# Two-block model on one core: squares of the norms added in pairs, one weighted moment for the final norm, and the first two units after a norm multiplied in parts

## The reference

```
y = x * rsqrt(mean(x*x) + EPS) * g            # EPS = 1e-6
h = y * (1 + scale) + shift                   # scale, shift from "ada" vectors
```

## Time and profile before

| quantity | value |
|---|---|
| median of 3 runs | 2177.64 us |
| the profiled execution, own time | 2177.91 us |
| its span (first to last instruction) | 2176.1 us |
| PE busy | 2119.0 us (97%) |
| DVE busy | 1749.7 us (80%) |
| ACT busy | 1334.7 us (61%) |
| mean granted TensorE clock | 0.988 |
| experts stage, from about | 1155 us |

### The profile page before, as it was taken

One profiled execution on the slowest core, in us unless ns is written; L12 is line 12 of the kernel. 1 busy time (PEld: TensorE's weight loads), 2 busy tenths in 40 slices (PEclk: granted clock), 3 DMA queues, 4 the chain that ended last, 5 costly groups with the idle time before them and its releaser, 6 DMA issues.

```text
span 2176.1 us, 33858 instructions
## 1 busy us (share of the span) xinstructions
PE 2119.0 (97%) x13613; PEld 1866.2 (86%) x13613; DVE 1749.7 (80%) x2143; ACT 1334.7 (61%) x1278; POOL 31.0 (1%) x60
## 2 busy tenths in 40 slices
PE   7999999999999999999999999999999999999998
PEld 5899999899999889999977888888888888888887
DVE  4978865877766878887878888888888888888887
ACT  3565554556645753434756776766777767776775
POOL 3000000000000000000000000000000000000000
PEclk8999999999999999999999999999999999999999
DMA  9777855566646548987456999999999999999995
GB/s 320 234 227 227 242 188 168 181 210 198 205 166 211 175 143 287 306 308 259 149 178 229 354 350 342 367 348 341 350 341 373 338 340 346 359 357 337 354 337 192
DMA packets 356160, 595.06 MB, mean 273 GB/s; under 512 B 10376, under 2 KB 201368, under 8 KB 356008
## 3 DMA queue, kind: packets, MB, share of 16 engines
q1 hardware_dynamic: 352864, 586.92, 78.7%
q0 software_dynamic: 2752, 5.86, 1.2%
q10 hardware_dynamic: 392, 0.13, 0.0%
HBM read 591.80 MB, written 4.22 MB: 274 GB/s over the span
## 4 chain that ended last, share of the span: by engine, by line
PE 83%; DVE 9%; ACT 3%; issue 3%; DMA 2%; SPq 0%; DVEq 0%; ACTq 0%
PE ps L1590 9%; PE ps L1592 9%; PE ps L1591 9%; PE ps L1119 6%; PE ps L1120 6%; PE ps L1121 6%; PE ps L1619 5%; PE ps L1620 5%; PE ps L1621 5%; PE ps L1144 2%; PE ps L1145 2%; PE ps L1146 2%; DVE wlo L1687 2%; DVE acc L1735 2%; ACT whi L701 1%
## 5 line engine op out<-in xcount | busy, mean ns | idle before, releaser
L1687 DVE TENSOR_TENSOR wlo<-raw,whi 128x2048 fp32r<-128x2048 f32 x485 | 1109.7, 2290 | 280.2 <-ACT whi L701 263.2
L701 ACT CAST whi<-raw 128x2048 fp32r<-128x2048 f32 x485 | 927.3, 1912 | 405.7 <-PE ps L1592 141.4
L1119 PE MATMUL ps<-hhi,whi 128*128 128x256 f32 x1424 | 411.3, 289 | 2.1 <-DVE wlo L1687 1.8
L1120 PE MATMUL ps<-hlo,whi 128*128 128x256 f32 x1424 | 403.4, 283 | 0.0
L1121 PE MATMUL ps<-hhi,wlo 128*128 128x256 f32 x1424 | 403.2, 283 | 0.0
L1590 PE MATMUL ps<-whi,xghi 128*128 128x512 f32 x896 | 364.1, 406 | 0.5 <-DVE wlo L1687 0.5
L1592 PE MATMUL ps<-wlo,xghi 128*128 128x512 f32 x896 | 353.9, 395 | 0.0
L1591 PE MATMUL ps<-whi,xglo 128*128 128x512 f32 x896 | 353.8, 395 | 0.0
L1119 PEld LDWEIGHTS ps<-hhi,whi 128*128 128x128 f32 x1424 | 273.5, 192 | 10.0 <-issue 7.0
L1120 PEld LDWEIGHTS ps<-hlo,whi 128*128 128x128 f32 x1424 | 273.6, 192 | 0.3
L1121 PEld LDWEIGHTS ps<-hhi,wlo 128*128 128x128 f32 x1424 | 273.4, 192 | 0.0
(11 more groups left out here) (381 smaller groups left out, 2987.9 us busy)
## 6 DMA issues: line engine op xcount, KB each, us to landing
raw<-in_moe_w_gate_dram SPq DMA_DIRECT2D x112, 1024.0 KB, 5.6
raw<-in_moe_w_up_dram SPq DMA_DIRECT2D x112, 1024.0 KB, 5.7
raw<-in_moe_w_down_dram SPq DMA_DIRECT2D x112, 1024.0 KB, 5.0
raw<-in_w_in_dram SPq DMA_DIRECT2D x92, 1024.0 KB, 5.3
raw<-in_w_ada_dram SPq DMA_DIRECT2D x69, 1024.0 KB, 7.8
raw<-in_w_out_dram SPq DMA_DIRECT2D x24, 1024.0 KB, 5.1
raw<-in_ffn_w_gate_dram SPq DMA_DIRECT2D x11, 1024.0 KB, 8.8
raw<-in_ffn_w_up_dram SPq DMA_DIRECT2D x11, 1024.0 KB, 8.3
```

The costliest lines, as they stand in the source:

```text
L701: nc.scalar.copy(whi[:, u.hl, :], raw[:, u.raw, :]).then_inc(hi_ready, 1)
L1119: mm(ps2[u.bank][:, j], whi[:, u.hl, w], hhi[:, k], start=k == 0, stop=False)
L1120: mm(ps2[u.bank][:, j], whi[:, u.hl, w], hlo[:, k], start=False, stop=False)
L1687: V.tensor_tensor(wlo[:, u.hl, :], raw[:, u.raw, :], whi[:, u.hl, :].bitcast(F32), ALU.subtract).then_inc(raw_free, 1)
```

## The change

1. **Pairs of squares.** In norms 1, 4, 5 and 6 (`ADDED`) VectorE adds tiles 0+1 and 2+3 of the squares, one instruction each, between the parts of the residual. TensorE sums 6 tiles and not 8.
2. **Final norm.** ScalarE no longer makes `gsq`. VectorE writes 8 matrices `gain2[k]` = g*g+EPS (128x128, the same in each column) ahead of the residual; TensorE uses them in place of `ones`, which gives the moment but for EPS*EPS, and that is the bias of Ln (`eps2`). VectorE adds up all squares in three instructions of 128x512 into two tiles `qsum`, and TensorE sums these for m. POOL's bias load and VectorE's clearing of `zpad` now wait for that last sum, because `gain2` and `qsum` lie in memory that they write.
3. **First two units together.** `norm` on VectorE does all 8 `norm_tile`, then all 8 `norm_low`. TensorE's `first_products` does, for u: both products with `hhi` by k; then the 16 hi*hi of v; the 16 hi*lo of u; then the 32 remaining ones of v. It is used behind norms 1, 3, 4 and 5; norm 0 keeps the old form with `products`, now without parts.
4. **One table load.** The set with Ln and Exp is loaded once, ahead of the last `high` before the norm; the two loads within the norm go.

```
+ADDED = (1, 4, 5, 6)
...
+        gain2, qsum = gsq[:, 0:KD // 2].rearrange("p k (a m) -> p (k a) m", a=2), gsq[:, KD // 2:KD // 2 + 2]
...
                 pool.wait_ge(t_ready, 8 * norm_no(N_MIX[l]) + 1)
+                if l == 0:
+                    pool.wait_ge(gain_sum_ready, 1)
...
+            def inverse_root(to, of, ready, value, least=eps, loaded=False):
                 n = to.shape[0]
-                nc.scalar.preload_act_table_set(LOG_EXP)
+                if not loaded:
+                    nc.scalar.preload_act_table_set(LOG_EXP)
...
             def norm_std(n):
-                nc.scalar.preload_act_table_set(LOG_EXP)
+                if n == 0:
+                    nc.scalar.preload_act_table_set(LOG_EXP)
...
-                    if n == N_FINAL:
-                        for k in range(2 * i, 2 * i + 2):
-                            last = nc.scalar.activation(gsq[:, k], xT[:, k], ACT.Square, scale=amul[:, N_FINAL, k:k + 1])
-                        last.then_inc(gain_squares, 1)
...
                 for j in range(OUT1_UNITS):
+                    if j == OUT1_UNITS - 1:
+                        nc.scalar.preload_act_table_set(LOG_EXP)
                     high(Unit(S_B1 + l * UNIT_L1 + H * HEAD_UNITS + j + LOOK))
...
+            def first_products(u, n):
+                v = u.plus(1)
+                def tile(of, k, j):
+                    return of[:, slice(256 * k + P * j, 256 * k + P * j + P)]
+                pe.wait_ge(raw_free, u.free())
+                for k in range(KD):
+                    pe.wait_ge(hhi_ready, KD * norm_no(n) + k + 1)
+                    for j in range(2):
+                        mm(ps2[u.bank][:, j], tile(whi[:, u.hl], k, j), hhi[:, k], start=k == j == 0, ...)
+                        mm(ps2[u.bank][:, j], tile(wlo[:, u.hl], k, j), hhi[:, k], start=False, ...)
+                pe.wait_ge(hi_ready, v.count())
+                for k in range(KD):
+                    for j in range(2):
+                        mm(ps2[v.bank][:, j], tile(whi[:, v.hl], k, j), hhi[:, k], start=k == j == 0, ...)
+                for k in range(KD):
+                    pe.wait_ge(hlo_ready, KD * norm_no(n) + k + 1)
+                    for j in range(2):
+                        last = mm(ps2[u.bank][:, j], tile(whi[:, u.hl], k, j), hlo[:, k], ...)
+                last.then_inc(unit_done, 1)
+                pe.wait_ge(raw_free, v.free())
+                for k in range(KD):
+                    for j in range(2):
+                        mm(ps2[v.bank][:, j], tile(whi[:, v.hl], k, j), hlo[:, k], ...)
+                        last = mm(ps2[v.bank][:, j], tile(wlo[:, v.hl], k, j), hhi[:, k], ...)
+                last.then_inc(unit_done, 1)
...
             def norm(n):                                            # TensorE
+                if n == N_FINAL:
+                    pe.wait_ge(gain_weights, 1)
                 for k in range(KD):
-                    if k % 2 == 0:
+                    if n in ADDED and k < 4:
+                        if k % 2:
+                            continue
+                        pe.wait_ge(squares_added, 2 * ADDED.index(n) + (3 if n > N_FINAL else 0) + k // 2 + 1)
+                    elif k % 2 == 0:
                         pe.wait_ge(squares, 4 * norm_no(n) + k // 2 + 1)
-                    last = mm(ps2[7][:, 0], ones[:, 0:P], h[:, k], start=k == 0, stop=k == KD - 1)
+                    last = mm(ps2[7][:, 0], gain2[:, k] if n == N_FINAL else ones[:, 0:P], h[:, k], ...)
...
             def norm(n):                                            # VectorE
-                back = 1
                 for k in range(KD):
                     norm_tile(n, k)
-                    if k >= back:
-                        norm_low(n, k - back)
-                for k in range(KD - back, KD):
+                for k in range(KD):
                     norm_low(n, k)
...
             def residual(n, last_unit, gate):
...
                     last.then_inc(x_ready, 1)
+                    if n in ADDED and 1 <= p < 3:
+                        dve.wait_ge(squares, 4 * norm_no(n) + p)
+                        V.tensor_tensor(h[:, 2 * p - 2], h[:, 2 * p - 2], h[:, 2 * p - 1], ALU.add).then_inc(squares_added, 1)
+                if n == N_FINAL:
+                    for p in range(1, 4):
+                        dve.wait_ge(squares, 4 * norm_no(n) + p + 1)
+                        if p > 1:
+                            dve.wait_ge(squares_added, 2 + p - 1)
+                        V.tensor_tensor(qsum, qsum if p > 1 else h[:, 0:2], h[:, 2 * p:2 * p + 2], ALU.add).then_inc(squares_added, 1)
...
+                    step(V.tensor_tensor(amul[:, N_FINAL], par2[...], par2[...], ALU.mult))
+                    for k in range(KD):
+                        last = V.tensor_scalar(gain2[:, k], ones[:, 0:P], amul[:, N_FINAL, k:k + 1], EPS, ALU.mult, ALU.add)
+                    last.then_inc(gain_weights, 1)
...
-            dve.wait_ge(sum_ready, norm_no(N_FINAL) + 1)
-            step(V.tensor_scalar(acc[:, 0], ps2[7][:, 0], EPS, EPS * EPS, ALU.mult, ALU.add))
-            dve.wait_ge(gain_sum_ready, 1)
-            V.tensor_tensor(acc[:, 0], acc[:, 0], ps2[6][:, 0], ALU.add).then_inc(moment_ready, 1)
             norm(N_MIX[0])
```

More of the change, by code:

```diff
@@ L701, in high @@
                 nc.scalar.copy(whi[:, u.hl, :], raw[:, u.raw, :]).then_inc(hi_ready, 1)
-            def inverse_root(to, of, ready, value, scale=1.0):
+            def inverse_root(to, of, ready, value, least=eps, loaded=False):
                 n = to.shape[0]
-                nc.scalar.preload_act_table_set(LOG_EXP)
+                if not loaded:
+                    nc.scalar.preload_act_table_set(LOG_EXP)
                 act.wait_ge(ready, value)
-                step(nc.scalar.activation(to, of, ACT.Ln, bias=eps[0:n], scale=scale))
+                step(nc.scalar.activation(to, of, ACT.Ln, bias=least[0:n]))
                 return nc.scalar.activation(to, to, ACT.Exp, scale=-0.5)
@@ L752, in norm @@
                     norm_high(N_MIX[0])
-                    act.wait_ge(sum_ready, norm_no(n) + 1)
-                    step(nc.scalar.activation(acc[:, 1], ps2[7][:, 0], ACT.Ln, bias=eps[:]))
+                    act.wait_ge(gain_sum_ready, 1)
+                    step(nc.scalar.activation(acc[:, 1], ps2[6][:, 0], ACT.Ln, bias=eps[:]))
                     nc.scalar.activation(acc[:, 1], acc[:, 1], ACT.Exp, scale=-0.5).then_inc(gain_std_ready, 1)
@@ L1151, in norm @@
             def norm(n):
+                if n == N_FINAL:
+                    pe.wait_ge(gain_weights, 1)
                 for k in range(KD):
-                    if k % 2 == 0:
-                        pe.wait_ge(squares, 4 * norm_no(n) + k // 2 + 1)
-                    last = mm(ps2[7][:, 0], ones[:, 0:P], h[:, k], start=k == 0, stop=k == KD - 1)
[L1156 to L1163, removed]
+                    if n in ADDED and k < 4:
[3 more added lines that the diff above has]
+                    elif k % 2 == 0:
+                        pe.wait_ge(squares, 4 * norm_no(n) + k // 2 + 1)
+                    last = mm(ps2[7][:, 0], gain2[:, k] if n == N_FINAL else ones[:, 0:P], h[:, k], start=k == 0, stop=k == KD - 1)
+                last.then_inc(sum_ready, 1)
+                if n == N_FINAL:
+                    pe.wait_ge(squares_added, 2 + 3)
+                    for k in range(2):
+                        last = mm(ps2[6][:, 0], ones[:, 0:P], qsum[:, k], start=k == 0, stop=k == 1)
+                    last.then_inc(gain_sum_ready, 1)
             def ada(a, bank):
@@ L1276, in _ @@
                         pe.wait_ge(taken_s, hd.count(7, -1))
-                    products(q, None if h_no else l)
+                    if l and not h_no:
+                        first_products(q, l)
+                    else:
+                        products(q, None if h_no else 0)
                     ada_after(0)
@@ L1281, in _ @@
                         pe.wait_ge(taken_s, hd.count(7, 0))
-                    products(k)
+                    if h_no or not l:
+                        products(k)
                     ada_after(1)
@@ L1432, in mixer @@
                         token_products(u)
-                    else:
-                        products(u, N_MIX[l] if j == 0 else None)
+                    elif j == 0:
+                        first_products(u, N_MIX[l])
+                    elif j > 1:
+                        products(u)
                     if j == 4:
@@ L1502, in _ @@
                     pe.wait_ge((fg_ready, fa_ready)[j % 2], j // 2)
-                products(Unit(S_FF + j), N_FFN[0] if j == 0 else None)
+                if j == 0:
+                    first_products(Unit(S_FF), N_FFN[0])
+                elif j > 1:
+                    products(Unit(S_FF + j))
                 if ada_beside_ff(j - 1) is not None:
@@ L2097, in mixer @@
                 low(Unit(first + 1))
+                if l == 0:
```

(1 more changed line is left out.)

30 lines of the change are left out of this document (20 added, 10 removed).

## The result

| | before | after |
|---|---|---|
| median, us | 2178.10 (4 runs, 2177.52 to 2179.36) | 2151.52 (4 runs, 2149.71 to 2152.19) |
| span of the profiled execution | 2176.1 | 2149.4 |
| ratio | | 0.9877, 95% interval 0.9865 to 0.9890 |

The account below looks back on a forecast made before the run. TensorE, busy 97% of the span, was taken as the bound. Norms 1, final, 4, 5, 6 gave 3.4 + 5.6 + 1.6 + 3.4 + 0 = 14.0 us off 2177.91; with 1.7 us expected clock cost, 2165.5 us, range 2161 to 2171.

Parts of the forecast that it names:

- moves as a block with its start: Experts' stage, nearly half the span: TensorE idle only 0.17 us in 200, so the stage just shifts with its start.
- My rival with the experts: Experts' loads and products fall out of step, 0.05 us more per unit, 17 us lost: 2181 us; chance 0.04.
- the term for norm 6: Norm 6: sum 0.8 us earlier, but the router's product waits for rb's load; gain 0, at most 1 us.
- norm 1: From norm 1's sums to the end of v: v ends at 374.0 instead of 377.4, gain 3.4 us, kept.
- final norm: Final norm with norm 3: TensorE gains 6.3 us, the tight mixer behind leaves 5.0 to 6.3; 5.6 taken.
- norm 4: Ahead of the feed-forward: v ends 3.3 us earlier, but a wait for ada leaves a gain of 1.6 us.
- norm 5: Same pattern as norm 1 with a second mixer behind: gain 3.4 us; a clock fall would cost up to 1.7.
- Sum of squares: Fewer sum records: Ln 0.81 us earlier at norm 1, 3.96 us at the final norm; no table load within norms.
- Parts: First two units: TensorE resumes on the first hhi; v's low gains 1.35 us at norm 1, arriving together with TensorE.
- VectorE's additions: Two additions of about 0.43 us fit the residual's gaps; qsum additions and gain2 (1.8 us) at the final norm stay hidden.
- The ada wait: Behind v at norm 4, TensorE newly waits some 1.7 us for VectorE's ada addition, which moves by only 1.35 us.
- my 1 in 2 at each: Behind norms 1 and 5 the clock falls with chance 1 in 2 each, costing up to 1.7 us; expected 1.7.

Follow-up runs that it names:

- b_shift: Kernel before, with one unused tensor of 32 bytes per partition behind eps and no other edit; 2160.1 us, ratio 0.9913.
- a_noshift: Changed kernel with eps2 in the same 32 bytes as eps, so every tensor lies where it lay before the change; 2167.6 us, ratio 0.9948.
- a_moe256: Changed kernel with the experts' tensors alone 256 bytes further; 2148.7 us, ratio 0.9864.
- a_oldprod: Changed kernel with first_products undone and VectorE's old order in norm, other three edits and layout kept; 2154.8 us.
- b_best: Kernel before with none of the edits, hhi and hlo behind cst, 32 unused bytes ahead of block 1, mixer and feed-forward tensors; 2148.0 us, ratio 0.9861.
- a_all32: Changed kernel with everything from raw on moved by 32 bytes, stationary and moving operands alike; 2150.9 us.
- a_thi32: Changed kernel with thi moved 32 bytes against the weights, and mg, ma and pick moved by 32 too; 2153.5 us.
- a_shift64: Changed kernel with 64 bytes more behind eps2, in front of acc and all that follows; 2167.5 us.

## Why the prediction was wrong

**The step that failed** is the sentence that the experts' stage "moves as a block with its start". I checked that stage for waits and loads, found none, and took the duration of its instructions as given. A changed allocation altered it: 20.4 us, more than the whole forecast. My rival with the experts had them fall out of step with their loads; the loads had no part in it (DMA share 0.98 before and 0.99 after, and b_shift gains the 20 us with no edit but 32 unused bytes). What sets the duration there is the position of a product's operands against each other.

**The rest of the sum held, in part by luck.** Measured without the shift, the change is worth 11.3 us; 12.4 were forecast (2177.9 - 2165.5). 2167.6 us lies in the range. But the term for norm 6 was wrong, and a_noshift's trace has 1.55 us there that the sum does not have, and 2.7 us lost ahead of norm 1, where next to nothing was changed.

| term | forecast | measured |
|---|---|---|
| norm 1 | 3.4 | 3.0 |
| final norm | 5.6 | 6.2 |
| norm 4 | 1.6 | 1.5; 1.4 in a_moe256 |
| norm 5 | 3.4, less a possible fall | 1.6 with a fall, 3.1 without |
| norm 6, to the end of the experts' first unit | 0 | 0.4; 1.0 to 1.1 at an equal clock |

- *Sum of squares.* 12 records; Ln stands 2.96 us behind the start of the sums, before 3.66: 0.7, forecast 0.81. At the final norm 3.65 for 7.63: 3.98, forecast 3.96. No load within a norm.
- *Parts.* TensorE resumes 1.17 us behind the first tile (forecast 1.13). The `low` of v ends 12.5 us behind the start of the sums (forecast 12.4), 0.3 before TensorE needs it: both arrive together. Start of sums to end of v: 16.8 (16.5) and 17.6 (17.2); of the missing 0.3 to 0.4, 0.15 is that TensorE resumed later behind the start of the sums, the rest that its 96 products took 11.75 us, not 11.5.
- *VectorE's additions* fit into the gaps (0.23 us stay idle), `qsum` ends 3.3 us behind the start of the sums (3.2), `gain2` takes 1.66 (1.8) and leaves 0.94 us of wait ahead of the residual: hidden.
- *Final norm.* All of TensorE's gain carried, 6.2 of at most 6.3. I had taken 5.6 because of VectorE's work ahead of the first scores. In a_noshift the mixer takes nothing back; in the changed kernel's execution it takes 0.6, of which 0.3 is the shift (b_shift loses as much there without an edit).
- *Norm 4.* The ada wait came where I put it, 1.34 us in a_moe256 (forecast 1.7). In the profiled execution a fall of the clock covers it, free as forecast.
- *The clock.* It fell once at norms 1 and 5, as my 1 in 2 at each had it (and 15 of 27 over all traces). What I missed: behind norm 1, at 389 to 403 us, the lower level lasted 10.2 us for 6.8 before, and 1.1 us is given back in these 14 us. This too is chance: b_shift, with none of the edits, has 10.2 and loses 1.2, and a_noshift and a_moe256 have 6.8 and lose nothing.
- *Norm 6.* The router's product did wait for `rb`, as I said, and starts no earlier: 6.47 us behind the start of the sums before, 6.64 after. But I took the start for the end. Before, its 16 matmuls come in as the tiles of `h` do; after, the tiles are 0.7 us earlier, and when the load lands most of them are there. The row before, then the row after:

```profile
1140.17 3.05 PE L1520 MATMUL ps<-h,wr 128*8 128x256 f32 x16 [2.85 <-ACT h L740]
1134.49 2.17 PE L1571 MATMUL ps<-h,wr 128*8 128x256 f32 x16 [3.72 <-DMA rb<-in_moe_b_router_dram]
```

  From the start of the sums to the end of the experts' first unit it is 24.4 us before and 24.0 after, where the clock was at its lower level for 13.7 us and before for 6.8. With 6.8 (a_oldprod) it is 23.3; with 3.4 it is 23.8 without the edits (b_best) and 22.8 with them (a_moe256). So the term that I put at 0 is worth 1.0 to 1.1 us.
- *Not forecast: the feed-forward*, which returns 3.1 us. With TensorE 7.6 us ahead ScalarE waits for weight loads, in the 70 us behind 800. Before:

```profile
ACT whi L701 <- DMA raw<-in_ffn_w_up_dram: 8.4, 4, 2.6
```

After, and with it TensorE for ada:

```profile
ACT whi L707 <- DMA raw<-in_ffn_w_up_dram: 12.4, 4, 4.8
```

```profile
PE ps L1211 <- DVE acc L1797: 1.4, 2, 0.9
```

This varies: a_all32, a_moe256, a_thi32 and a_shift64, with the same instructions, lose 0.2 to 0.3 us against the kernel before where this execution lost 2.2 (units 107 to 112), so I call the loads its likely cause, not a shown one. Over the whole feed-forward the loss is 0.4 us in a_thi32 and 2.0 to 3.0 in the other three (in a_moe256 and a_shift64 the ada wait behind norm 4 is part of it).

- *Not forecast: the output projections* became slower by 0.6 us per 8 units in block 1, which is the same shift with the other sign (118.4 to 119.9 ns).

## What to carry to other kernels

A diff's allocations are part of the change: list which operands move against which, also for stages whose code is untouched, before taking their durations over. Where TensorE is the bound, try its layout by itself, with unused bytes alone; here that was worth 30 us and cost nothing. And when an edit gains less than its place shows, compare stretches of several traces: falls of the clock and waits of 1 to 3 us that come and go elsewhere can hide a gain of the size of `first_products`. A product that waits for one input may still end with another: follow its last matmul, not its first.

## What the runs showed of the hardware

- Float32r products, weights loaded for each: with 512 moving columns the step is 226.7 to 227.4 ns if stationary and moving operand start at the same byte modulo 256, and 231 to 233.3 if the stationary one lies 32 bytes ahead or behind, 64 or 128 behind (a_thi32's products of `tlo` excepted, which are slow at equal positions beside slow neighbours). With 256 columns it is the reverse: 120 ns at equal positions, 116.8 with the moving one 32 bytes behind, 117.6 with 64, 118.4 with 32 ahead.
- The Trainium skill, "SBUF — State Buffer", section "Who interferes with whom", gives TensorE two independent read ports, one for the moving operand and one for weights, and says that TensorE never waits on anyone. The runs have nothing on the latter as far as other engines are meant. They do not bear out the independence of the two in time: with nothing else changed, the distance between the two operands sets the step (233.2 or 227.4 ns). By which mechanism no run here tells; distances under 32 bytes were not tried.
- With the same instructions and the same 2.17 us of idle time behind the sums of norm 5, the granted clock fell to 0.50 (the 1.2 GHz level) in the changed kernel's execution and stayed at 1.00 in those of a_all32 and a_moe256. Over norms 1, 4 and 5 of all traces it fell in 15 of 27 places with that idle time, and in none of 6 with 0.44 us.
